# Two side places for the first expert, the second bias in the third pair, another order in the last pair

## The reference, cut to what matters

```python
h = x + hybrid_mixer(rms_norm(x), ...)           # three branches, gated, times w_out
logits = rms_norm(h) @ w_router + b_router       # top 4 of 32, softmax of these: gates
# for each expert e and the tokens routed to it:
u = x_e @ w1[e] + b1[e]                          # 1024 -> 2048
a = min(glu, 7) * sigmoid(1.702 * min(glu, 7)) * (clip(lin, -7, 7) + 1)
y = a @ w2[e] + b2[e]                            # 1024 -> 1024
h = h + gate * y ; out = rms_norm(h) * final_norm_w
```

## Time and profile before

| | us |
|---|---|
| median of 3 runs | 1287.34 |
| lowest, highest | 1286.79, 1288.43 |
| the profiled execution | 1288.56 |
| its span, first to last instruction | 1286.30 |
| TensorE busy (matmuls), share of the span | 1211.1, 94% |
| VectorE, ScalarE busy | 370.6, 184.7 |
| 16 DMA engines: data, mean rate | 449.26 MB, 349 GB/s |
| in the chain that ended last: TensorE, loads, VectorE | 63%, 31%, 4% |

### The profile page before, as it was taken

How to read it: one execution, slowest core, us unless ns; L and a number is a source line. 1 busy time by engine, 2 the same in 40 slices (tenths; PEclk the granted TensorE clock), 3 DMA queues, 4 the chain that set the end, 5 groups by cost and what they waited for, 6 DMA issues and landing times.

```text
span 1286.3 us, 15495 instructions
## 1 busy us (share of the span) xinstructions
PE 1211.1 (94%) x6550; PEld 591.9 (46%) x6550; DVE 370.6 (29%) x629; ACT 184.7 (14%) x357; POOL 0.2 (0%) x4
## 2 busy tenths in 40 slices
PE   9999999999999999999998989898998989898986
PEld 7886788888543333333332323232333323232322
DVE  2158452411142233131331313122223313131223
ACT  2225521200120000100011000000010010100002
POOL 0000000000000000000000000000000000000000
PEclk9999999999999999999999999999999999999999
DMA  9354212695489999999999999999999999999995
GB/s 360 108 170 132 66 35 67 213 396 217 150 297 418 429 428 427 428 426 428 426 429 425 431 427 430 428 427 431 425 431 425 431 425 431 427 429 430 426 427 212
DMA packets 52131, 449.26 MB, mean 349 GB/s; under 512 B 5584, under 2 KB 18000, under 8 KB 26864
## 3 DMA queue, kind: packets, MB, share of 16 engines
q1 hardware_dynamic: 51744, 447.49, 84.3%
q10 hardware_dynamic: 336, 1.05, 0.3%
HBM read 447.48 MB, written 1.05 MB: 349 GB/s over the span
## 4 chain that ended last, share of the span: by engine, by line
PE 63%; DMA 31%; DVE 4%; issue 1%; ACT 1%; SPq 0%; DVEq 0%; PEldq 0%; ACTq 0%
PE ps L485 62%; DMA ring<-in_w_exp 19%; DMA upper<-in_w_exp 11%; PE ps L1021 1%; DVE ring L1485 1%; PE ps L746 0%; DMA xrows<-in_x 0%; DVE ring L1588 0%; DVE upper L1569 0%; ACT ring L1131 0%; DVE ring L1482 0%; PE ps L1032 0%; PE ps L652 0%; DVE upper L1524 0%; ACT upper L1197 0%
## 5 line engine op out<-in xcount | busy, mean ns | idle before, releaser
L485 PE MATMUL ps<-ring,upper 128*64 128x512 f32 (+4 forms) x2688 | 516.5, 527 | 30.6 <-DMA ring<-in_w_exp 26.3
L485 PE MATMUL ps<-upper 128*64 128x512 f32 (+5 forms) x1836 | 329.2, 461 | 23.4 <-DMA upper<-in_w_exp 15.8
L485 PEld LDWEIGHTS ps<-ring,upper 128*64 128x64 f32 (+2 forms) x2688 | 165.4, 136 | 340.3 <-issue 295.1
L485 PEld LDWEIGHTS ps<-upper 128*64 128x64 f32 (+3 forms) x1836 | 152.3, 154 | 191.4 <-issue 161.0
L485 PE MATMUL ps<-xT,ring 128*128 128x256 f32 x672 | 150.5, 381 | 0.4 <-DVE xT L1446 0.4
L485 PEld LDWEIGHTS ps<-xT,ring 128*128 128x128 f32 x672 | 126.1, 190 | 18.7 <-issue 1.1
L1752 DVE TENSOR_TENSOR upper<-ps,merged 128x512 f32<-128x512 f32 x32 | 22.1, 692 | 352.6 <-PEq L995 352.6
L1773 DVE TENSOR_TENSOR xrows<-xrows,ps 128x1024 f32<-128x1024 f32 x30 | 36.6, 1222 | 296.6 <-PE ps L485 296.6
L1349 ACT ACTIVATE xT<-upper 128x512 f32<-128x512 f32 x32 | 20.2, 631 | 544.9 <-DVE upper L1755 544.9
L1355 ACT ACTIVATE factors<-ps 64x512 f32<-64x512 f32 x63 | 37.3, 592 | 238.5 <-PEq L1016 237.7
L485 PE MATMUL ps<-factors,cst 128*128 128x512 f32 x128 | 63.2, 617 | 1.0 <-DVE factors L1832 1.0
(11 more groups left out here) (227 smaller groups left out, 491.8 us busy)
## 6 DMA issues: line engine op xcount, KB each, us to landing
ring<-in_w_exp SPq DMA_DIRECT2D x124, 2048.0 KB, 37.3
upper<-in_w_exp SPq DMA_DIRECT2D x63, 2048.0 KB, 37.3
ring<-in_w_exp SPq DMA_DIRECT2D x10, 1024.0 KB, 36.5
ring<-in_w_gate SPq DMA_DIRECT2D x9, 1024.0 KB, 5.2
ring<-in_w_in SPq DMA_DIRECT2D x8, 896.0 KB, 12.0
ring<-in_w_in SPq DMA_DIRECT2D x8, 640.0 KB, 4.0
ring<-in_w_branch SPq DMA_DIRECT2D x5, 1024.0 KB, 5.1
ring<-in_w_mem_kv SPq DMA_DIRECT2D x4, 1024.0 KB, 5.0
```

Source lines behind the costliest of these rows:

```text
L485: return pe.matmul(o, l, r, start=start, stop=stop, skip_group_check=True)
```

## The change

1. `SIDE = 2`: chunks c=6 and c=7 of expert 0's first layer don't go to the ring but to two places of their own, `side`: `kb(52, 8)` and `xT`. Each is loaded by `load_side`, c=7 after SyncE has waited for the last gate (`gate_ps`), c=6 after it has waited for the router (`logit_ps`), behind the loads of the first layer of expert 1 and the second of expert 0. TensorE waits for them by `side_full` and doesn't add to `slots_used` for them. All later chunks stand two places earlier. `actT`, `sel`, `selg` and `b2rows` change places with each other's memory for that.
2. The second bias moves from the first pair to the third: its products come after c=2 and c=5 of expert 4's first layer, VectorE adds them before `swiglu` of expert 4. In the first pair `gather` of the second pair moves ahead of expert 1's first layer. ScalarE loads `b2rows` when expert 0's first layer is done, and `finw` after the first sigmoid.
3. The last pair has a function of its own on TensorE: second layer of 29, first of 30 (with the scatters of the pair before), first of 31 in banks 4 and 5 (with the transposes of expert 30 after c=2), second of 30, second of 31. The loads follow that order. The last 1 MB is loaded as two halves, each with a semaphore of its own. VectorE and ScalarE follow.

Besides, `sinks` counts on `lora_loaded`, and loops over groups run one turn fewer, with the last group written out. The diff, cut (blank lines are left out too):

```diff
+SIDE = 2
+PASS = NE * CPE - SIDE
...
-        b2rows = kb(68, 4)
+        b2rows = kb(56, 4)
...
+        side = (kb(52, 8), xT_flat)
...
-        def w1_place(c, q, a, r, zero):
-            return place(q, a, r * CPE + c if zero else r * CPE + c - 4)
-        def w2_place(i, q, a, r, final):
-            return place(q, a, r * CPE + i + (8 if final else 16))
+        def w1_place(c, q, a, r, zero, swapped=False):
+            if swapped:
+                return place(q, a, r * CPE + c - SIDE)
+            return place(q, a, r * CPE + c if zero else r * CPE + c - (4 + SIDE))
+        def w2_place(i, q, a, r, final, swapped=False):
+            return place(q, a, r * CPE + i + (8 if final or swapped else 16) - SIDE)
...
-            sp.dma_start(b2rows[0:NE, :], b_exp2[0]).then_inc(late_loaded, 16)
...
+                for c in range(0, KC - SIDE if zero else KC, 2):
+                    s, _, n = w1_place(c, q, a, r, zero, swapped)
...
+                    if final and i == 3:
+                        for cc in range(2):
+                            sp.dma_start(slot(s)[:, cc * D:(cc + 1) * D], src[:, :, j + cc, :].rearrange("p a f -> p (a f)"))\
+                              .then_inc(slot_full[s + 2 * cc], 16)
+                    elif fine:
...
+            def load_side(c):
+                j = c % 4
+                sp.dma_start(side[c - (KC - SIDE)], w_exp1[0, 0, 512:1024, :].rearrange("(p c) f -> p c f", c=4)[:, j, :]).then_inc(side_full, 16)
+            def load_group(q, a, very_first=False, zero=False):
                 for r in range(GROUP):
                     load_w1(q, a, r + 1, False, very_first and r == 0)
                     load_w2(q, a, r, 0 if very_first and r == 0 else 4)
+                    if zero and r == 0:
+                        if very_first:
+                            sp.wait_ge(logit_ps, TT)
+                        load_side(KC - 2)
+            def load_last_group(q):
+                for r in range(GROUP - 1):
+                    load_w1(q, GROUPS - 1, r + 1)
+                    load_w2(q, GROUPS - 1, r)
+                load_w2(q, GROUPS - 1, GROUP - 1, 4, False, True)
+                load_w1(q, GROUPS - 1, GROUP, False, False, True)
             def load_pass(q, very_first=False):
                 load_w1(q, 0, 0, True, very_first)
                 if very_first:
-                    load_group(q, 0, True)
-                with sp.Fori(1 if very_first else 0, GROUPS) as a:
+                    sp.wait_ge(gate_ps, len(UNITS))
+                load_side(KC - 1)
+                load_group(q, 0, very_first, True)
+                with sp.Fori(1, GROUPS - 1) as a:
                     load_group(q, a)
+                load_last_group(q)
                 load_w1(q, GROUPS, 1)
                 load_w2(q, GROUPS, 0, 2)
                 load_w2(q, GROUPS, 1, 0, True)
...
-            def up(q, a, r, E, N, parity, between, zero=False):
+            def up(q, a, r, E, N, parity, between, zero=False, bank=0, swapped=False):
                 for c in range(KC):
-                    s, times, n = w1_place(c, q, a, r, zero)
+                    aside = zero and c >= KC - SIDE
                     if parity == 0 and c % 4 == 0:
                         pe.wait_ge(xg_sb, N * 2 + c // 4 + 1)
-                    if c % 2 == 0:
-                        pe.wait_ge(slot_full[s], times * 16 + 16 * uses[s])
+                    if aside:
+                        weights = side[c - (KC - SIDE)]
+                        if c == KC - SIDE:
+                            pe.wait_ge(side_full, q * (16 * SIDE) + 16 * SIDE)
+                    else:
+                        s, times, n = w1_place(c, q, a, r, zero, swapped)
+                        weights = slot(s)
+                        if c % 2 == 0:
+                            pe.wait_ge(slot_full[s], times * 16 + 16 * uses[s])
                     for z in range(2):
                         for hf in range(2):
-                            last = mm(ps[64 * hf:64 * hf + 64, z, :], xg[:, c, parity * SLOTS:(parity + 1) * SLOTS],
-                                      slot(s)[:, hf * D + z:(hf + 1) * D:2], c == 0, c == KC - 1)
-                    last.then_inc(slots_used, 1)
+                            last = mm(ps[64 * hf:64 * hf + 64, bank + z, :], xg[:, c, parity * SLOTS:(parity + 1) * SLOTS],
+                                      weights[:, hf * D + z:(hf + 1) * D:2], c == 0, c == KC - 1)
+                    if not aside:
+                        last.then_inc(slots_used, 1)
                     if between:
                         between(c)
-                pe.wait_ge(slots_used, n + (NMIX + 1))
-                pe.sem_inc(up_ps, 1)
-            def down(q, a, r, E, whole=4, final=False, between=None, very_first=False):
+                if zero:
+                    last.then_inc(up_ps, 1)
+                else:
+                    pe.wait_ge(slots_used, n + (NMIX + 1))
+                    pe.sem_inc(up_ps, 1)
+            def down(q, a, r, E, whole=4, final=False, between=None, very_first=False, swapped=False):
...
+                        if final and k == 7:
+                            pe.wait_ge(slot_full[s + 2], odd_full(s + 2, q))
...
+            def turn_gates(N, first=False, biased=False):
                 pe.wait_ge(selg_sb, N + 1)
-                if first:
-                    pe.wait_ge(b2_sb, 2)
-                else:
+                if biased:
+                    pe.wait_ge(b2_sb, TT)
+                if not first:
                     pe.wait_ge(acc_sb, N * 2)
...
+                    pe.wait_ge(acc_sb, TT)
+                    pe.wait_ge(rows_loaded, 16)
...
+            def pair(q, a, p, first, turn_wait=None):
                 E, N, r = q * NE + a * GROUP + 2 * p, q * NPAIR + a * (GROUP // 2) + p, 2 * p
-                very_first, second = turn_wait == "first", turn_wait == "second"
+                very_first, second, third = turn_wait == "first", turn_wait == "second", turn_wait == "third"
                 if not very_first:
                     pe.wait_ge(up_read, E)
-                up(q, a, r, E, N, 0, turn_all_gates if very_first else None, first)
+                def bias_between(c):
+                    if c in (2, 5):
+                        second_bias(c // 5)
+                up(q, a, r, E, N, 0, turn_all_gates if very_first else bias_between if third else None, first)
                 if not first:
                     down(q, a, r - 1, E - 1)
                 if very_first:
-                    second_bias(0)
+                    gather(N + 1)
                 else:
                     turn(E)
@@ -1073,10 +1122,8 @@
                     if first:
                         if very_first and c == 0:
                             turn(E)
-                        elif very_first and c == 3:
-                            second_bias(1)
                     elif c == 0:
-                        turn_gates(N - 1, second)
+                        turn_gates(N - 1, second, third)
                     elif c == 2:
                         scatter(N - 1, 0)
                     elif c == 5:
@@ -1084,17 +1131,40 @@
                 pe.wait_ge(up_read, E + 1)
                 up(q, a, r + 1, E + 1, N, 1, between)
-                def turns(i):
+                if not very_first:
+                    gather(N + 1)
+                down(q, a, r, E, 0 if very_first else 4, False, None, very_first)
+                turn(E + 1)
+            def last_pair(q):
+                E, N = q * NE + NE - 2, q * NPAIR + NPAIR - 1
+                def scatters(c):
+                    if c == 0:
+                        turn_gates(N - 1)
+                    elif c == 2:
+                        scatter(N - 1, 0)
+                    elif c == 5:
+                        scatter(N - 1, 1)
+                def turn_even(c):
+                    if c == 2:
+                        turn(E)
+                def turn_odd(i):
                     if i == 2:
                         turn(E + 1)
-                        turn_gates(N, False)
-                if last:
-                    down(q, a, r, E, 2, False, turns)
-                else:
-                    gather(N + 1)
-                    down(q, a, r, E, 0 if very_first else 4, False, None, very_first)
-                    turn(E + 1)
+                        turn_gates(N)
+                down(q, GROUPS - 1, GROUP - 1, E - 1, 4, False, None, False, True)
+                pe.wait_ge(up_read, E)
+                up(q, GROUPS - 1, GROUP, E, N, 0, scatters, False, 0, True)
+                up(q, GROUPS, 1, E + 1, N, 1, turn_even, False, 4)
+                down(q, GROUPS, 0, E, 2, False, turn_odd)
+                down(q, GROUPS, 1, E + 1, 0, True)
+                scatter(N, 0, 6, True)
+                scatter(N, 1, 0, True)
...
-            act.dma_start(finw, final_norm_w.unsqueeze(0).to_broadcast([P, D])).then_inc(late_loaded, 16)
...
+                if very_first:
```

(52 more changed lines are left out.)

42 lines of the change are left out of this document (18 added, 24 removed).

## The result

| | before | after |
|---|---|---|
| median, us | 1287.74 (14 runs) | 1290.26 (14 runs) |
| lowest, highest | 1286.79, 1289.93 | 1289.72, 1291.35 |
| ratio after to before, 95% interval | | 1.0019 (1.0012 to 1.0026) |
| span of the profiled execution | 1286.3 | 1288.0 |

The changed kernel is 2.5 us slower. I had forecast 1.1 us faster, with a range up to 1288.7, so the time lies outside it and on the other side. The loads went much as forecast. The traces show time lost in two places that no term of my sum covered: after the last store, and in the first 10 us.

The account below looks back on a forecast made before the run. The prediction took the gapless stream of expert loads at about 428 GB/s as the bound. Span 1286.30 - 0.5 (stream) + 0 (bias) - 0.6 (ending) = 1285.2, so median 1287.34 - 1.1 = 1286.2 us; range 1283.7 to 1288.7.

Parts of the forecast that it names:

- The ending behind it is unchanged: After the last matmul: everything up to the kernel's end was to take as long as before, with no term in the sum.
- the prediction's own signs of being wrong: Transfers running through 387 to 391 us without a hole, or a last landing over 2 us earlier than 1271.5.
- The layer of expert 0 ends at 379.9 us as now: First expert's first layer on TensorE: it was to end at the same time as before the change.
- the hole: Expert loads around 387 to 391 us: transfers idle 2 to 5 us until expert 1's c=1 frees places at 388.4.
- The lead: How much earlier loads land in the full stream after the first experts: 0 to 1.4 us, taken as 0.5.
- The last of the 20 chunks: Prefetch before the first expert: the last chunk, asked for at 360.0 us, was to land about 366 us.
- The 395.3 us: Landing of the load behind the idle stretch, using about 2.0 us fixed cost; the prediction's range was 395.6 to 397.1.
- The rival of an expensive empty queue: Loads after the idle stretch start slowly: 1289.7 us, or 1291.2 with a third load that pays; chance 0.10.
- Part 2: Second bias to the third pair, gather ahead: 0 us at the end; 1.5 us slower without the idle stretch as cover.
- Part 3: Last pair's new order and halved last chunk: TensorE ends 0.6 us sooner, at most 1.0; last landing unchanged.

Follow-up runs that it names:

- Moving one line: The changed kernel with SyncE's wait for the stores moved behind its skip over the code of further passes: 1288.07 us, ratio 1.0006 to the kernel before.
- padding the kernel before: The kernel before with SyncE's code for further passes doubled, code that never runs: 1289.57 us, ratio 1.0016.
- the sister kernels: The follow-up kernels made from the changed one by further edits; those that keep its new last order measured 1285.60 to 1290.48 us.
- the kernel of all that paid: Changed kernel with SyncE's late wait, gather back, expert 1 in banks 6 and 7, transposes after its c=2, old last order: 1284.16 us, ratio 0.9974.
- the two kernels that return to the loop: Old order in the last pair, on the changed kernel with the late wait (1286.42 us) and on the kernel with the transposes later (1284.16 us).
- the kernel with TensorE's group written out: The kernel before with SyncE's late wait and TensorE's last group of six experts written out behind the loop: 1289.67 us, ratio 1.0011.
- the kernel with the transposes later: Changed kernel with late wait, gather back, expert 1 in its own banks, expert 0's transposes after expert 1's c=2: 1285.60 us, ratio 0.9989.

## Why the prediction was wrong

- **The step that failed: a term put at nothing.** "The ending behind it is unchanged", says the prediction of what lies behind the last matmul. SyncE's skip over unneeded passes belongs to it; the change makes its code longer and the skip went from 0.5 to 2.7 us. Moving one line gave back 2.2 us, and padding the kernel before took 2.1. The rows for it were in the trace of the kernel before (branch at 1285.5, last step at 1286.0, both in view above). I read the chain of waits, which stops at VectorE's last operation at 1282.2, and counted the last group written out behind its loop as no cost. Of the prediction's own signs of being wrong none came: they looked at the loads and at TensorE alone.
- **The start failed too.** "The layer of expert 0 ends at 379.9 us as now" has no term for the code's size. The profiled start is 0.6 us late, in the sister kernels up to 1.4. Together, with the profile's own numbers: start and stream +0.5 at the last landing, -0.8 of TensorE's lag, -0.2 at the stores, +2.2 skip = +1.7 in the span. The medians say +2.5, with an interval from 1.5 to 3.3. The two profiled runs differ by 1.2 in device time (1289.73 against 1288.56), since that of before was 0.8 above its median and that of after 0.5 below; where the medians' other 1.3 us are no trace shows. Beside the experiments the kernel before had median spans of 1285.4 to 1285.7, so the 1286.3 of its trace is late for it.
- **Part 1, the hole: mechanism right, the digits partly luck.** Expert 1's c=1 was forecast to free the load at 388.4 and did at 388.8 (388.1 without the late start); the landing behind the hole was to be 395.6 to 397.1 and was 396.2; the fourth after it 415.2 to 416.7 and was 416.9. The lead was forecast at 0.5 and is 0.4 to 0.6, but kernels that load as before scatter from -1.3 to 0.8, so agreement to 0.1 us is chance. The split was off: I put 4.4 us into the hole and it cost 2.3. The loads ahead of it were later than forecast (377.8, 382.7 and 389.0 us against at most 377.3, 382 and 387), partly by ScalarE's loads. The last of the 20 chunks landed at 368.0, not 366, with no effect. The 395.3 us that the prediction works out for the landing behind the hole with the fixed cost of the Trainium skill (DMA: Bandwidth & Descriptors, Anatomy of one DMA) is an estimate that lies below its own range, not "within the above", and that section is about loads issued by GpSimd, while these are SyncE's; the load took 7.5 us, 2.6 beside its transfer. The rival of an expensive empty queue fell: the loads after the hole came 4.9, 6.0, 4.9 and 4.9 us apart.
- **Part 1, its reading as two separate edits: off.** I saw the gather's 1.9 us in the load's issue, but not what it was worth: with the gather back and the waits for VectorE taken away the same side places give 2.9. Nor did I see that TensorE's next wait, for VectorE ahead of the transposes, would take the gather's place.
- **Part 2: right.** The traces show no cost in the third pair: the steady rate of the loads is unchanged. ScalarE's loads, issued at 380.5 and 382.2, delayed the load before the hole (issued at 376.9, it lands 6.3 us behind the one before it) and the hole swallowed it. Without the hole, in the kernel of all that paid, two loads land 6.1 and 5.7 us apart and not 4.9: 2.0 us where I had put 1.5, though a thin queue may have part in the second. The Trainium skill (DMA: Bandwidth & Descriptors, Issuing engines are not separate DMA queues) says that they share the transfer engines; this trace agrees, with that gap of 6.3 instead of 4.9 us.
- **Part 3: size right, split wrong.** Forecast 0.6, measured 0.8 us less lag, mostly from the two halves. The order itself brings 0.2 and its written-out code costs more than that: without it the kernel is 1.65 us faster.

## What to carry to other kernels

Read the trace to its last instruction, also behind the end of the chain of waits: here a branch over code that isn't needed took 0.5 us with little code and 2.7 with more, and most of that is hidden if it runs before the wait for the last stores and not after. Writing out a loop's last turn is an edit with a price of its own: 1.8 us on TensorE alone, with the same instructions in the same order, and 1.4 to 1.65 us came back in the two kernels that return to the loop. More places for prefetch help only as long as they come free early enough: a place that frees nothing when used moves the idle time of the loads, and one has to look at which use frees the next one and what stands before it on its engine.

## What the runs showed of the hardware that I had not expected

- SyncE's step over unneeded code took 0.5 us in the kernel before and 2.7 us in the changed one and in the one padded with code that never runs. VectorE's took 3.2 us in the kernel before.
- With more TensorE code in the program, run or not, a load issued at 1.7 us landed 0.5 to 1.6 us later (5.8 to 6.0 us against 6.6 to 7.5), in 8 of 8 kernels against 6 of 6, one trace each.
- In the trace of the kernel with TensorE's group written out the first expert starts 2.9 us later than before, though the transposes start only 1.3 later: from 11.0 to 13.2 us the granted clock was 0.67 (mean of the stretch, between the full and the half level), where the kernel before has 1.00. TensorE had been busy for 1.13 of the 3 us before. That doesn't explain it, since the kernel with the transposes later has the same 1.13 us and a clock of 1.00 behind. It is also the slowest of that kernel's 11 runs, 2.0 us above the median, so how often this happens is open. The stretches of the kernel written out, then of the one with the transposes later:

```profile
8.00:11.00 3.00, 1.13 (x9) 0.86 (x8) 1.71 (x6) 0.80 (x3) 0.00 (x0) 1.00 1.01 423
11.00:13.20 2.20, 1.82 (x5) 1.53 (x6) 2.20 (x7) 0.00 (x0) 0.00 (x0) 0.67 0.98 411
13.20:20.00 6.80, 6.80 (x28) 5.78 (x27) 1.21 (x4) 2.48 (x5) 0.00 (x0) 0.85 1.02 407
```

```profile
8.00:11.00 3.00, 1.13 (x9) 0.86 (x8) 1.87 (x7) 0.65 (x3) 0.00 (x0) 1.00 1.00 401
11.00:13.20 2.20, 1.98 (x9) 1.80 (x10) 2.20 (x7) 0.00 (x0) 0.00 (x0) 1.00 0.99 414
```
